# Rearranged gates, sums of squares and norm weights in a three-mixer transformer step on one core

## The reference

```python
def rmsnorm(x, w):
    xf = x.astype(jnp.float32)
    y = xf * lax.rsqrt(jnp.mean(xf * xf, axis=-1, keepdims=True) + EPS)
    return (y * w.astype(jnp.float32)).astype(x.dtype)
...
def rglru(x, w_a, b_a, w_x, b_x, lam):
    r = sigmoid(einsum(xb, w_a) + b_a); i = sigmoid(einsum(xb, w_x) + b_x)
    log_a = -LRU_C * r * softplus(-lam)
    u = jnp.sqrt(-jnp.expm1(2.0 * log_a)) * (i * x)
    h[t] = exp(log_a[t]) * h[t - 1] + u[t]
```

## Time and profile before

| | |
|---|---|
| median of 3 runs | 3475.65 us (3473.97 to 3477.48) |
| profiled execution, own time | 3474.76 us |
| its span | 3472.6 us |
| mean granted clock of TensorE | 0.959 |
| TensorE busy | 93% of the span |
| VectorE, ScalarE, GpSimd busy | 67%, 53%, 20% |

### The profile page before, as it was taken

How to read it: one execution, slowest core, us unless ns; L and a number is a source line. 1 busy time by engine, 2 the same in 40 slices (tenths; PEclk the granted TensorE clock), 3 DMA queues, 4 the chain that set the end, 5 groups by cost and what they waited for, 6 DMA issues and landing times.

```text
span 3472.6 us, 54222 instructions
## 1 busy us (share of the span) xinstructions
PE 3231.7 (93%) x21710; PEld 2944.0 (85%) x21710; DVE 2320.0 (67%) x3235; ACT 1833.2 (53%) x2370; POOL 687.3 (20%) x1118
## 2 busy tenths in 40 slices
PE   6999878999999899998998988998999999999998
PEld 6889878888888888887877877888999888888887
DVE  7655767656666776667666766666656788888544
ACT  5544667544665555654555444333444566666443
POOL 2000000010000000012676775776000100000000
PEclk9999988999999999999999999988999999999999
DMA  5435333555444445555433333333555555555554
GB/s 189 141 134 180 126 109 132 191 188 195 163 156 156 151 152 174 173 188 199 158 105 115 129 121 121 132 131 128 199 184 183 188 192 189 189 191 191 188 188 140
DMA packets 158046, 560.54 MB, mean 161 GB/s; under 512 B 17552, under 2 KB 25808, under 8 KB 157152
## 3 DMA queue, kind: packets, MB, share of 16 engines
q1 hardware_dynamic: 157792, 557.06, 47.6%
HBM read 550.64 MB, written 6.36 MB: 160 GB/s over the span
## 4 chain that ended last, share of the span: by engine, by line
PE 68%; DVE 12%; POOL 10%; ACT 6%; issue 3%; DMA 1%; DVEq 0%; ACTq 0%; POOLq 0%; SPq 0%
PE ps L555 68%; POOL TB L1906 5%; DVE WL L1309 3%; POOL PT L1906 2%; ACT WH L890 2%; POOL BX L1906 2%; ACT L880 1%; POOL BS L1906 1%; POOL SQ L1906 1%; DVE XV L1283 1%; DVE XC L1283 1%; DVE BS L1299 0%; DVE X L1283 0%; DMA RAW<-in_w 0%; ACT SQ L880 0%
## 5 line engine op out<-in xcount | busy, mean ns | idle before, releaser
L555 PE MATMUL ps<-XN,WH 128*128 128x256 f32 (+1 forms) x8864 | 1901.3, 308 | 54.2 <-DVE XN L1272 20.0
L890 ACT ACTIVATE WH<-RAW 128x1024 fp32r<-128x1024 f32 x1010 | 1065.1, 1058 | 1309.2 <-PE ps L555 1276.8
L1309 DVE TENSOR_TENSOR WL<-RAW,WH 128x1024 fp32r<-128x1024 f32 x1010 | 1260.9, 1253 | 518.7 <-ACT WH L890 512.4
L555 PEld LDWEIGHTS ps<-XN,WH 128*128 128x128 f32 x8864 | 1468.2, 197 | 144.8 <-issue 22.2
L555 PE MATMUL ps<-XN,WL 128*128 128x256 f32 x5120 | 1461.8, 285 | 0.0
L555 PEld LDWEIGHTS ps<-XN,WL 128*128 128x128 f32 x5120 | 999.8, 195 | 0.0
L555 PE MATMUL ps<-YS,WH 128*128 128x512 f32 (+1 forms) x1088 | 377.7, 392 | 31.6 <-DVE ZB L1272 29.4
L1906 POOL TENSOR_TENSOR RSB<-RSB,SQ 128x256 f32<-128x256 f32 x75 | 87.5, 1166 | 1244.1 <-ACT SQ L880 1243.1
L555 PE MATMUL ps<-YS,WL 128*128 128x256 f32 x1056 | 296.5, 281 | 0.0
L555 PEld LDWEIGHTS ps<-YS,WH 128*128 128x128 f32 x1088 | 203.9, 190 | 81.9 <-DVE ZB L1272 32.3
L1906 POOL TENSOR_TENSOR SQ<-SQ 128x256 f32<-128x256 f32 (+1 forms) x32 | 37.8, 1182 | 1129.5 <-ACT SQ L880 1127.5
(11 more groups left out here) (327 smaller groups left out, 3423.3 us busy)
## 6 DMA issues: line engine op xcount, KB each, us to landing
RAW<-in_w SPq DMA_DIRECT2D x1010, 512.0 KB, 3.3
CSB<-sums SPq DMA_DIRECT2D x64, 128.0 KB, 3.7
scratch<-X SPq DMA_DIRECT2D x2, 2048.0 KB, 7.8
X<-scratch SPq DMA_DIRECT2D x2, 2048.0 KB, 7.7
X<-in_x SPq DMA_DIRECT2D x4, 512.0 KB, 7.9
X<-in_x SPq DMA_DIRECT2D x1, 2048.0 KB, 7.9
out<-X SPq DMA_DIRECT2D x4, 512.0 KB, 2.6
WIF<-in_w_if SPq DMA_DIRECT2D x1, 576.0 KB, 14.3
```

The lines of the kernel that those rows point to most:

```text
L555: return pe.e.matmul(dst, l, r, start=start, stop=stop, skip_group_check=True)
L890: act.e.activation(WH[:, w % NH, :], RAW[:, w % NB, :], ACT.Copy).then_inc(*act.one(("wh", w)))
L1309: dve.e.tensor_tensor(WL[:, w % NB, :], RAW[:, w % NB, :], WH[:, w % NH, :].bitcast(F32), SUB).then_inc(*dve.one(("wl", w)))
```

## The change

In all four norms ScalarE rounds X times the norm weight in one instruction (its scale operand), and VectorE makes the remainder as X times weight minus high part in one instruction; TMP goes, and for oo the product of both weights (FW) is made once. In the recurrence, the gates of pair q-1 come after the first xl tile of pair q, two gate tiles share a PSUM bank, the forced ends of xl and zl go, and tail(q-1) runs until the end of pair q. The chain ssd has 20 steps: GpSimd's folding is at 13, TensorE's sum at 15, the root at 16, scaling at 17, rounding at 18, the remainder at 19, and its `End` comes after the second zs tile of the next group. In gla and diff GpSimd's addition goes: TensorE adds both halves with two accumulating products. The store of X waits for the sums of the out projection and no longer for the multiplied tile.

```diff
-    "tail": 6, "heads": 64, "eo": 1, "dt": 1, "dts": 6, "xv": 1, "zs": 1, "ssd": 16, "oo": 1, "nx": 4,
+    "tail": 6, "heads": 64, "eo": 1, "dt": 1, "dts": 6, "xv": 1, "zs": 1, "ssd": 20, "oo": 1, "nx": 4,
...
-    for q in range(8):
-        for i in range(2):
-            p.append(whole(tile("xl", (2 * q + i,), "e_w_in", 128 * (2 * q + i)), 16))
-        for i in range(2):
-            p.append(whole(tile("zl", (2 * q + i,), "e_w_in", 4096 + 128 * (2 * q + i)), 16))
-        p += [End("xl", (2 * q + 1,)), End("zl", (2 * q + 1,))]
+    for q in range(9):
+        if q < 8:
+            p.append(whole(tile("xl", (2 * q,), "e_w_in", 128 * (2 * q)), 16))
         if q:
-            p.append(End("tail", (q - 1,)))
-        for kind, w in (("ra", "e_lru_wa"), ("ix", "e_lru_wx")):
+            for kind, w in (("ra", "e_lru_wa"), ("ix", "e_lru_wx")):
+                for i in range(2 * q - 2, 2 * q):
+                    p.append(whole(tile(kind, (i,), w, (i, 0), "lru"), 1))
+            p.append(Go("tail", (q - 1,)))
+        if q < 8:
+            p.append(whole(tile("xl", (2 * q + 1,), "e_w_in", 128 * (2 * q + 1)), 16))
             for i in range(2):
-                p.append(whole(tile(kind, (2 * q + i,), w, (2 * q + i, 0), "lru"), 1))
-        p.append(Go("tail", (q,)))
+                p.append(whole(tile("zl", (2 * q + i,), "e_w_in", 4096 + 128 * (2 * q + i)), 16))
+            if q:
+                p.append(End("tail", (q - 1,)))
...
-        if g:
-            p.append(End("ssd", (g - 1,)))
-        else:
+        if g == 0:
...
                 p.append(Go("ssd", (g,)))
+            if j == 1 and g:
+                p.append(End("ssd", (g - 1,)))
...
-                if s == 13:
+                if s == 15:
                     b = take("side", "y2s", g)
                     pe.wait_ge(*at("ysq", g))
...
                     b = take("side", "gn", h)
-                    pe.wait_ge(*at("gsq", h))
-                    mm(b[:, 0:256], ones, SQ[:, 0, 0:256]).then_inc(*pe.one(("gn", h)))
+                    pe.wait_ge(*at("gsqr", h))
+                    mm(b[:, 0:256], ones, SQ[:, 0, 0:256], True, False)
+                    mm(b[:, 0:256], ones, SQ[:, 0, 256:512], False, True).then_inc(*pe.one(("gn", h)))
...
+            def norm_tile(L, k, x):
+                fn(XN[:, k, 0:256], x[:, k, :], ACT.Copy, ("xh", L, k), scale=norm_w(L, k))
+                square(("sqr", L), k, RSB, 0, x[:, k, :])
                 if L == 2:
-                    act.wait_ge(*at("xf", L, k))
-                    square(("sq1r", L), k, RS1, 2, tmp[:, k % 2, :])
-                act.wait_ge(*at("xw", L, k))
-                fn(XN[:, k, 0:256], tmp[:, k % 2, :], ACT.Copy, ("xh", L, k))
-                square(("sqr", L), k, RSB, 0, x[:, k, :])
+                    square(("sq1r", L), k, RS1, 2, x[:, k, :], cv("final_norm", k))
...
+                if j % 2:
+                    act.wait_ge(*at("tile", "ra", j))
+                    if j > 1:
+                        act.wait_ge(*at("lruscan", j // 2 - 1))
+                    for i in range(2):
+                        fn(RB[:, i, :], bank("ra", j - 1)[:, 256 * i:256 * i + 256], ACT.Sigmoid, ("free", "ra", j - 1),
+                           bias=cv("lru_ba", j - 1 + i))
...
-            def norm_rest(L, k, tmp):
+            def norm_rest(L, k, x):
                 dve.wait_ge(*at("xh", L, k))
-                rest(XN[:, k, :], tmp[:, k % 2, :], ("xn", L, k))
+                stt(XN[:, k, 256:512], x[:, k, :], norm_w(L, k), XN[:, k, 0:256].bitcast(F32), MUL, SUB, ("xn", L, k))
...
-            def gla(h, s):
-                if s == 12:
-                    pool.wait_ge(*at("gsqr", h))
-                    tt(SQ[:, 0, 0:256], SQ[:, 0, 0:256], SQ[:, 0, 256:512], ADD, ("gsq", h))
...
-                sp.wait_ge(*at("xw", 1, 15))
+                sp.wait_ge(*at("xa", 1, 15))
```

More of the change, by code:

```diff
@@ L363, in build @@
         EPSC = fx("epsc", 1)
+        FW = fx("FW", 16)
         R0 = fx.at
@@ L527, in cs, with norm_w @@
             return CS[rows, SOFF[name] + c:SOFF[name] + c + (n or w)]
+        def norm_w(L, k):
+            return FW[:, k:k + 1] if L == 2 else cv(["e_norm", "o_norm", "", "norm_ffn"][L], k)
         ident, ones = cs("ident"), cs("ones")
@@ L594, in block @@
                 id_ = (t.kind,) + t.args
-                if start:
+                if start and t.x == "lru" and t.args[0] % 2:
+                    open_[id_] = open_[t.kind, t.args[0] - 1]
+                elif start:
                     open_[id_] = [take("main", *id_)]
@@ L609, in block @@
                     h, l = WH[:, u % NH, b * 128:b * 128 + 128], WL[:, u % NB, b * 128:b * 128 + 128]
-                    dst = banks[0][:, 0:256]
+                    c = 256 * (t.args[0] % 2) if t.x == "lru" else 0
+                    dst = banks[0][:, c:c + 256]
                     mm(dst, h, x[:, 0:256], start, False)
@@ L859, in diff @@
                     b = take("side", "dnm", h)
-                    pe.wait_ge(*at("dsq", h))
-                    mm(b[:, 0:256], ones, SQ[:, 0, 0:256]).then_inc(*pe.one(("dnm", h)))
+                    pe.wait_ge(*at("dsqr", h))
+                    mm(b[:, 0:256], ones, SQ[:, 0, 0:256], True, False)
+                    mm(b[:, 0:256], ones, SQ[:, 0, 256:512], False, True).then_inc(*pe.one(("dnm", h)))
             def last():
@@ L890, in unit, with square @@
                     act.e.activation(WH[:, w % NH, :], RAW[:, w % NB, :], ACT.Copy).then_inc(*act.one(("wh", w)))
-            def square(key, n, acc, slot, x):
+            def square(key, n, acc, slot, x, scale=1.0):
                 if n == 0:
-                    fn(acc, x, ACT.Square, (*key, 0))
+                    fn(acc, x, ACT.Square, (*key, 0), scale=scale)
                 else:
@@ L897, in square, with project @@
                         act.wait_ge(*at(key[0][:-1], key[1], n - 2))
-                    fn(SQ4[:, slot + n % 2, :], x, ACT.Square, (*key, n))
-            def norm_tile(L, k, x, tmp):
+                    fn(SQ4[:, slot + n % 2, :], x, ACT.Square, (*key, n), scale=scale)
+            def norm_tile(L, k, x):
+                fn(XN[:, k, 0:256], x[:, k, :], ACT.Copy, ("xh", L, k), scale=norm_w(L, k))
+                square(("sqr", L), k, RSB, 0, x[:, k, :])
                 if L == 2:
-                    act.wait_ge(*at("xf", L, k))
-                    square(("sq1r", L), k, RS1, 2, tmp[:, k % 2, :])
-                act.wait_ge(*at("xw", L, k))
-                fn(XN[:, k, 0:256], tmp[:, k % 2, :], ACT.Copy, ("xh", L, k))
-                square(("sqr", L), k, RSB, 0, x[:, k, :])
-            def norm0(k):
-                norm_tile(0, k, X0, TMP0)
+                    square(("sq1r", L), k, RS1, 2, x[:, k, :], cv("final_norm", k))
+            def norm0(k):
+                act.wait_ge(*at(f"x0{k // 4}"))
+                norm_tile(0, k, X0)
+            def project(L, kind, n):
+                act.wait_ge(*at("xa", L, n))
+                norm_tile(L, n, X)
             def rsqrt(dst, src, n, *names):
@@ L995, in ra @@
             def ra(j, s):
[L996 to L999, removed]
-            def ix(j, s):
-                act.wait_ge(*at("tile", "ix", j))
-                fn(IB[:, j % 2, :], bank("ix", j)[:, 0:256], ACT.Sigmoid, ("ixd", j), ("free", "ix", j),
-                   bias=cv("lru_bx", j))
+                if j % 2:
[5 more added lines that the diff above has]
+                           bias=cv("lru_ba", j - 1 + i))
+            def ix(j, s):
+                if j % 2:
+                    act.wait_ge(*at("tile", "ix", j))
+                    for i in range(2):
+                        fn(IB[:, i, :], bank("ix", j - 1)[:, 256 * i:256 * i + 256], ACT.Sigmoid, ("ixd", j),
+                           ("free", "ix", j - 1), bias=cv("lru_bx", j - 1 + i))
             def tail(p, s):
@@ L1511, in heads, with project @@
                     rest(YS1[:, 16 + 4 * h:20 + 4 * h, :], HB, ("ysh", h))
-            def project(L, kind, n, load, w):
+            def project(L, kind, n, load):
                 dve.wait_ge(*at("tile", kind, n))
@@ L1516, in project @@
                 tt(X[:, n, :], X[:, n, :], bank(kind, n)[:, 0:256], ADD)
-                tt(X[:, n, :], X[:, n, :], bank(kind, n)[:, 256:512], ADD, ("free", kind, n))
-                norm_tile(L, n, X, TMP, w)
+                tt(X[:, n, :], X[:, n, :], bank(kind, n)[:, 256:512], ADD, ("free", kind, n), ("xa", L, n))
+                if n:
+                    norm_rest(L, n - 1, X)
+                if n == 15:
+                    norm_rest(L, n, X)
             def eo(n, s):
-                project(1, "eo", n, "x1", "o_norm")
+                project(1, "eo", n, "x1")
             def dt(s):
```

47 lines of the change are left out of this document (16 added, 31 removed).

## The result

The kernel after takes 3366.88 us (median of 4 runs, 3358.37 to 3368.05) where the kernel before took 3476.06 beside it: a ratio of 0.968 (0.967 to 0.969), 109 us less. The forecast was 3353.7 us, between 3300 and 3402. The profiled execution took 3367.36 us with a span of 3365.6, and the following rows are read against it.

The account below looks back on a forecast made before the run. TensorE, busy for 93% of the span, was taken as the bound, so only its stops and slow clock could be won. -54 - 40 - 23 - 5 = -122 from 3474.8, plus 0.9 to the median, gave 3353.7 us; range 3300 to 3402.

Parts of the forecast that it names:

- State space sums, -54: State space groups: sending TensorE two units later removes seven SQ stops, 30 us, plus clock time; between -40 and -55.
- the 22 us put down to the clock: State space groups: time won from the lowered clock, at most 23, since most lowered stretches are tied to the SQ stops.
- Gates, -40: Recurrence: of 75 us in stops and slow clock, 40 go, leaving it near VectorE's busy time; ends -15 and -75.
- VectorE would be busy for 98%. It is the next bound: Recurrence: with 75 us taken from 280, 205 are left, against VectorE's 201.8 us busy, so VectorE limits the gain.
- also waits for, in order: Recurrence: VectorE's waits for IB 15.2, EM 9.5 and TH 9.3, 34.0 us; if all stay, at least 236 us remain.
- Attention sums, -23: Attention heads in the branches: stops -24, GpSimd's dropped work -2, TensorE's added products +3; between -3 and -39.
- the -24 for the stops that are won: Branches: of 32 us of SQ stops, 12 of 14, 8 of 9.2 and half of the other 9 are won.
- Norm tiles, -5: Start of the kernel: less VectorE work on the normed input shortens XN's waits, 7 us winnable; between 0 and -7.
- (a): Rival, chance 0.20: the recurrence comes down to TensorE's own time, -75 instead of -40; 3318.7 us.
- (b): Rival, chance 0.22: stops move to WL and HH; the recurrence gives 15, the attention sums 3; 3398.7 us.
- (c): Rival, chance 0.04: the state space sums are still late, squares coming over 2.1 us later than now; 3405.7 us.
- (d): Rival, chance 0.03: slower, as VectorE and ScalarE work in turns in the recurrence, 393 us instead of 280; 3506.7 us.

Follow-up runs that it names:

- sum14: Kernel after, with TensorE's sum of squares of the state space groups at step 14 instead of 15; 3378.44 us, 11.6 us slower than after.
- no_tables: hh_later with the recurrence's and its heads' sigmoids, silus, tanhs, logarithms and exponentials replaced by squares, 42 of 44 table loads gone, results wrong; 3298.38 us.
- only_attn_sums: Kernel before with only the attention sums changed, TensorE adding both halves; 3457.68 us, ratio 0.9944.
- hh_later: Kernel after, with TensorE's products on s5's HH one unit later (step 7, not 6) and VectorE's use of their sum at step 8; 3320.03 us.
- pad64: Kernel before plus an unused 64-byte tile in front of the big tiles, where the change has FW; 3464.98 us against 3479.59, ratio 0.9963.
- only_norms: Kernel before with only the norm tiles of the change; 3467.3 us against 3477.36, ratio 0.9967.

## Why the prediction came out as it did

The time was inside the range, 13 us above the forecast; the sum hides errors of both signs.

- **State space sums, -54: right.** The stage lost 49.3 us, a group takes 474.9 / 7 = 67.8 us where 67 was said, no SQ stop is left in them, and with the stops' 30 came 19 of the 22 us put down to the clock. Part of the rest is a stop of 2.2 us on YS ahead of the last blocks of oo, for which 0 to 2 was left. sum14 shows the arithmetic of units at work: one unit less brings back 1.4 us a stop where it gives 1.1.
- **Gates, -40: right in size by luck, wrong in its bound.** The stage lost 36.0 us, which taken from 280 leaves 244; RB went, and WL and EB stand where ZB stood. The step that failed is "VectorE would be busy for 98%. It is the next bound": it is busy for 199.6 of 250 us, and in no_tables the same VectorE does its work in a recurrence 22 us shorter still. The row with the answer was cited there: what VectorE "also waits for, in order", 34 us, all of it ScalarE's. It was not all that VectorE waited for: the largest line of that list, 20.5 us for the rounded weights WH, also ScalarE's, was left out:

```profile
DVE WL L1309 <- ACT WH L890: 20.5, 12, 3.5
```

  The same view after, 334 to 584 us:

```profile
DVE WL L1329 <- ACT WH L901: 12.7, 10, 3.1
DVE TH L1292 <- ACT TH L891: 6.9, 4, 2.5
...
DVE IB L1292 <- ACT IB L891: 4.5, 2, 2.2
...
DVE EB L1292 <- ACT EM L891: 1.2, 2, 0.9
```

  Of the 34.0 us, 12.6 stayed, and by the prediction's row the stretch would have come to 201.8 + 12.6 = 214 us. That it came out at 244, near the forecast, is luck. The engine to be asked was ScalarE, and its table loads. The Trainium skill (ScalarE: Activation LUTs, Table sets) says to batch activations by table set; no run here batches them, but leaving 42 loads out was worth 22 us. It also says that one set holds the logarithm and the exponential; the trace differs, with four loads between these two in the heads' roots of this stretch alone, and the measurement decides.
- **Attention sums, -23: too much here.** In the full change the stage lost 11.4 us, alone the part gave 20. The mechanism was right ("GpSimd's lateness is not gone; s5 needs it at the next HH"): SQ's 32 us went, HH gained 4 stops and 6.3 us where one or two more stops were said. What was mis-sized is the -24 for the stops that are won. All stops of TensorE in the windows above, 85.3 us before, are 69.3 after, so 16 were won: besides HH, DOS gained 4.4 us, and the waits for ScalarE's squares are 2.5, the longest 1.8 where under 1.5 was said. TensorE's busy time grew by 5.5 us (720.6 to 726.1), of which the sum has 3 to 5 for the products of ones. In only_attn_sums the stops were 65.7 us and the busy time 718.2; why the two kernels differ by 8 us there stays open. hh_later shows that the lateness wanted one unit, as in the state space groups.
- **Norm tiles, -5: right at the start, and a term was missing.** VectorE's remainders took 9.0 us for 16, in the range of 7.8 to 15.5, and XN's stops fell from 20.0 to 17.7; the start is 3.5 us shorter. But FW, costed at 0 as "one small instruction", moved every large tile behind it by 64 bytes, and pad64 shows that this alone is worth 9 to 17 us. Whether the norm edit itself gives anything beyond its start, the runs cannot tell: only_norms and pad64 have nearly the same ratio.
- **Rivals.** (a), the recurrence at TensorE's own time, did not happen: 36 us of its 75. no_tables comes within some 17 us of it, but leaves the loads out. (b), the stops move, happened in part in the branches, where 16 of SQ's 32 us came back; in the recurrence EB and WL stop TensorE, but for less than half of the 44 us before, so that it gave 36 and not 15. (c) and (d) did not happen; but taking turns, (d)'s mechanism, is what is left in the recurrence, at a price of a few us per pair.

The two profiled executions differ by 107.4 us, 15 less than the 122 of the sum: 5 in the groups, 4 in the recurrence and 12 in the attention heads are missing, and a gain of some 6 from addresses and small stages was not in it.

## What to carry to other kernels

Where a stop recurs and the releaser was busy in time, convert its length into steps of the hand-written order first: one or two units later for the consumer removed 30 us of stops and 49 us of time here, and 47 us of time at another place that the change had not touched. An engine with a high busy share beside a late one is not yet the bound: take its work away or take the other's away, and see which moves the end. And before a small gain is put down to an edit, run the old kernel with nothing but the edit's new tile.

## What was not expected of the hardware

- The step between products depends on where the operands lie in SBUF: 233 or 230 ns with 512 columns, 120 or 117 with 256, for shifts of 32 or 64 bytes, worth 9 to 17 us of 3480 in one case and 10 to 14 in another. The runs show that the address matters, not which rule it follows.
- ScalarE's table loads, 1.283 us each, are 154 in the kernel after, 198 us of its 1841. A stretch of 288 us has 44 of them; leaving 42 out made the recurrence 22 us shorter, though ScalarE was busy for only 75% of it.
- Seven stops of 1.4 us left the granted clock of their stretch at 1.00; seven of 4.3 us went with 0.96, 15 HH stops of 2.7 us on average with 0.93.
